# Two transformer blocks with a mixture of experts on one core: norm weights by ScalarE's DMA queue, x turned bank by bank, an expert loader that waits on the work itself, and a gate moved to GpSimd

## The reference

```python
h = rms_norm(x, attn_norm_w)
c_q, c_kv, k_rope, dq, dk, dv, g_mla, g_diff = split(h @ w_in)      # widths 256,256,32, then five times 1024
o_mla  = attention(16 heads, from rms_norm(c_q) @ mla_w_uq and rms_norm(c_kv) @ mla_w_ukv)
o_diff = rms_norm(differential_attention(8 heads, rms_norm(dq), rms_norm(dk), dv), diff_subln_w) * 0.2
merged = sigmoid(g_mla + b1) * o_mla + sigmoid(g_diff + b2) * o_diff
x = x + merged @ w_out
# 16 experts; each takes the 32 tokens that score highest for it
hidden = silu(xe @ w_gate[e]) * (xe @ w_up[e])                      # 1024 -> 2048, xe is 32 rows
x = x + scatter(hidden @ w_down[e] * gate)
# second block
proj = rms_norm(x, norm1_g_2) @ w_in_2      # convolution part, 8 heads of stick-breaking attention, gating unit
y_c = gelu(c_u) * (tril(sgu_w) @ rms_norm(gelu(c_v), sgu_norm_g))   # the gating unit
x = x + concat(y_conv, y_attention, y_c) @ w_out_2
x = x + square(relu(rms_norm(x) @ w_ff1_2)) @ w_ff2_2
x = x + sigmoid(rms_norm(x) @ w_ple_gate_2) * (p_2 @ w_ple_proj_2)
```

## Time and profile before

| | |
|---|---|
| median of 3 runs | 1473.36 us |
| profiled execution | 1473.55 us, of which the span of the core is 1471.8 us |
| PE busy | 1129.7 us, 77% |
| DVE busy | 468.1 us, 32% |
| ACT busy | 374.7 us, 25% |
| POOL busy | 49.0 us, 3% |
| DMA read | 491.52 MB, 335 GB/s over the span |

### The profile page before, as it was taken

One profiled execution on the slowest core, in us unless ns is written; L12 is line 12 of the kernel. 1 busy time (PEld: TensorE's weight loads), 2 busy tenths in 40 slices (PEclk: granted clock), 3 DMA queues, 4 the chain that ended last, 5 costly groups with the idle time before them and its releaser, 6 DMA issues.

```text
span 1471.8 us, 20240 instructions
## 1 busy us (share of the span) xinstructions
PE 1129.7 (77%) x8437; PEld 684.3 (46%) x8437; DVE 468.1 (32%) x879; ACT 374.7 (25%) x623; POOL 49.0 (3%) x107
## 2 busy tenths in 40 slices
PE   9999999965656566656656657566566999999998
PEld 8887887521212212212112122122121688999887
DVE  6988885100000000000000000000000478675546
ACT  6658663100001001001001000000100465465434
POOL 1220120000000000000000000000000020000000
PEclk9999999997878968888798687886887999999999
DMA  8663528999999999999999999999999764555551
GB/s 307 200 245 108 206 87 370 420 426 427 427 426 430 428 428 427 427 429 427 426 430 428 427 427 427 428 428 427 430 427 428 294 186 172 172 184 189 196 186 47
DMA packets 58922, 493.33 MB, mean 335 GB/s; under 512 B 6715, under 2 KB 8309, under 8 KB 34165
## 3 DMA queue, kind: packets, MB, share of 16 engines
q1 hardware_dynamic: 58724, 492.07, 82.4%
q10 hardware_dynamic: 144, 0.52, 0.1%
HBM read 491.52 MB, written 1.05 MB: 335 GB/s over the span
## 4 chain that ended last, share of the span: by engine, by line
DMA 54%; PE 40%; DVE 3%; ACT 1%; issue 1%; SPq 0%; ACTq 0%; DVEq 0%
DMA arena<-in_expert_w_down 19%; DMA arena<-in_expert_w_up 18%; DMA arena<-in_expert_w_gate 17%; PE ps L1927 13%; PE ps L2020 7%; PE ps L1932 7%; PE ps L2374 4%; PE ps L2398 2%; PE ps L1999 1%; PE ps L2190 1%; PE ps L2221 1%; DVE w_split L1199 1%; PE ps L1897 1%; PE ps L2134 1%; PE ps L2109 1%
## 5 line engine op out<-in xcount | busy, mean ns | idle before, releaser
L2374 PE MATMUL ps<-ring,arena 128*32 128x512 f32 x1024 | 168.3, 793 | 115.5 <-DMA ring<-in_expert_w_up 60.1
L2374 PE MATMUL ps<-arena 128*32 128x512 f32 x1024 | 163.2, 772 | 115.4 <-DMA arena<-in_expert_w_up 58.6
L1199 DVE TENSOR_TENSOR w_split<-ring,w_split 128x1024 fp32r<-128x1024 f32 (+3 forms) x178 | 201.9, 1141 | 93.6 <-ACT w_split L765 92.3
L765 ACT ACTIVATE w_split<-ring 128x1024 fp32r<-128x1024 f32 (+3 forms) x178 | 175.2, 991 | 180.5 <-PE ps L1932 126.8
L1651 DVE TENSOR_TENSOR arena<-arena,ps 128x512 f32<-128x512 f32 x16 | 11.0, 688 | 557.8 <-PE ps L2374 557.8
L2374 PEld LDWEIGHTS ps<-ring,arena 128*32 128x32 f32 x1024 | 32.9, 127 | 241.5 <-DMA ring<-in_expert_w_up 101.1
L2374 PEld LDWEIGHTS ps<-arena 128*32 128x32 f32 x1024 | 32.7, 126 | 236.0 <-DMA arena<-in_expert_w_up 96.1
L2020 PE MATMUL ps<-hT_hi,w_split 128*128 128x256 f32 x608 | 111.8, 284 | 0.5 <-ACT w_split L765 0.4
L2398 PE MATMUL ps<-arena 128*32 128x256 f32 x1072 | 81.2, 455 | 32.9 <-DMA arena<-in_expert_w_down 27.8
L2398 PE MATMUL ps<-ring,arena 128*32 128x256 f32 x896 | 69.9, 465 | 43.1 <-DMA ring<-in_expert_w_down 40.1
L2020 PEld LDWEIGHTS ps<-hT_hi,w_split 128*128 128x128 f32 x608 | 95.3, 192 | 2.3 <-issue 1.0
(11 more groups left out here) (360 smaller groups left out, 1379.0 us busy)
## 6 DMA issues: line engine op xcount, KB each, us to landing
ring<-in_expert_w_up SPq DMA_DIRECT2D x36, 2048.0 KB, 36.2
arena<-in_expert_w_gate SPq DMA_DIRECT2D x35, 2048.0 KB, 35.6
ring<-in_expert_w_gate SPq DMA_DIRECT2D x28, 2048.0 KB, 35.9
arena<-in_expert_w_up SPq DMA_DIRECT2D x28, 2048.0 KB, 37.2
arena<-in_expert_w_down SPq DMA_DIRECT2D x25, 2048.0 KB, 37.1
ring<-in_expert_w_down SPq DMA_DIRECT2D x21, 2048.0 KB, 37.1
ring<-in_w_ff SPq DMA_DIRECT2D x32, 1024.0 KB, 5.0
ring<-in_w_in SPq DMA_DIRECT2D x23, 1024.0 KB, 5.0
```

Of the source, the lines that this page charges most:

```text
L765: act.activation(w_split[:, n % WBUFS, 0, 0:cols], slot_view(slot, cols)[:, n % 2, :], ACT.Copy).then_inc(split_hi, 1)
L1199: dve.tensor_tensor(buf[:, 1, :], w, buf[:, 0, :].bitcast(F32), ALU.subtract).then_inc(split_lo, 1)
L2374: m = pe.matmul(ps[j * CAP:(j + 1) * CAP, bank, :], xe[:, kt, :], w[r][:, j * FCOL:(j + 1) * FCOL], start=kt == 0, stop=kt == KT - 1, skip ...
```

## The change

- The norm weight of the first product is loaded by ACT's DMA queue, as its first instruction, and no longer by SP between x and the first weights. PE turns it ahead of x, and turns x bank by bank (both halves of tokens of a bank, then the next bank) and not half by half.
- ACT writes `hT_hi` 0 and 1 before the first weight tile is split, then alternates. DVE likewise.
- The turning of the other weight vectors moves from between `c` and `dq` to behind the fourth tile of `dq`; their copies on DVE move behind `low_parts("dq", 3, 5)`.
- `low_parts("uq0", 0, 1)` moves ahead of the angle computation, and the sum of 2048 squares of `dq` on DVE is cut into two with `low_parts("uq1", 1)` between them.
- `gate_outputs` leaves DVE. POOL does it, as an addition and a multiplication of 1024 elements for each of two column halves.
- SP waits on PE's results themselves (`hO_done`, `tr_done`) for six of the first chunks; PE's waits for its own results go. Chunk 2 is loaded as two parts: 3072 of its 4096 columns once the last head is turned (`hT_done`), the rest once the last head is done.
- The first half of chunk 12 is loaded as two quarters, each freed by its own two matrix products.
- In the gating unit the square moves from ACT to POOL, and ACT splits weight tile 2 of `conv` in its place, ahead of the sigmoids of head pair 0.

```diff
-T1_RELEASES = SLOTS - 2
+T1_RELEASES = 4
+        KEYS, KEY_WORDS = 2, 3072
+        all_heads, merged = (hO_done, DHEADS + HEADS), (tr_done, 4 * TRANSPOSED.index("merge") + 4)
+        FREED_BY = {0: (hO_done, DHEADS), 1: (hO_done, DHEADS + IN_GROUP), KEYS: all_heads, LAST_ARENA: all_heads,
+                    3: merged, HALVED: merged}
...
-                    sp.wait_ge(first_half_used, 1)
-                    sp.dma_start(slot[:, 0:WIDE // 2], source[:, 0:WIDE // 2]).then_inc(first_half_loaded, 16)
+                    for i in range(2):
+                        words = slice(i * WIDE // 4, (i + 1) * WIDE // 4)
+                        sp.wait_ge(first_quarter_used, i + 1)
+                        sp.dma_start(slot[:, words], source[:, words]).then_inc(first_quarters_loaded, 16)
...
+            sp.wait_ge(hT_done, DHEADS + HEADS)
+            sp.dma_start(expert_slot(KEYS)[0][:, 0:KEY_WORDS], chunk_source(0, KEYS)[:, 0:KEY_WORDS]).then_inc(keys_loaded, 16)
...
# POOL
-            pool.sem_inc(od_ready, 1)
+            for c in range(2):
+                pool.wait_ge(gate_ready, HALVES + c + 1)
+                g, od = (b[:, :, c * 512:(c + 1) * 512] for b in (gb, dq))
+                step(pool.tensor_scalar(g, g, 1.0, None, ALU.add))
+                pool.tensor_tensor(od, od, g, ALU.mult).then_inc(od_gated, 2)
...
+            pool.wait_ge(gelu_done, 4)
+            pool.wait_ge(sq_read, 7)
+            gating = cv2.rearrange("p h d -> p (h d)")
+            pool.tensor_tensor(sq[:, 0:HALVES * SGU], gating, gating, ALU.mult).then_inc(sq_ready, 1)
...
# ACT
-            high_parts("c", 0, 2)
+            act.dma_start(vec_rows[0:KT, :], t["attn_norm_w"][0].rearrange("(r c) -> r c", c=P)).then_inc(norm_w_loaded, 16)
             act.wait_ge(vec_ready, 1)
-            high_stage("attn", 0, "attn_norm_w")
+            high_stage("attn", 0, "attn_norm_w", range(0, 2))
+            high_parts("c", 0, 1)
+            high_stage("attn", 0, "attn_norm_w", range(2, 4))
+            high_parts("c", 1, 2)
+            high_stage("attn", 0, "attn_norm_w", range(4, KT))
...
-            act.activation(sq[:, 0:HALVES * SGU], cv2.rearrange("p h d -> p (h d)"), ACT.Square).then_inc(sq_ready, 1)
+            high_parts("conv", 2, 3)
...
# DVE
             low_parts("dq", 3, 5)
+            dve.wait_ge(vec_done, 2)
+            dve.tensor_copy(vec[:, KT:NVEC], ps[:, 6, KT:NVEC]).then_inc(vec_ready, 1)
...
-            diff_sums(0)
+            dve.wait_ge(sq_ready, 1)
+            step(dve.tensor_reduce(ss_d[:, 0:HEADS], sq[:, 0:D].rearrange("p (n d) -> p n d", d=DQK), AX, ALU.add))
             low_parts("uq1", 1)
+            head_sums(0, sq[:, D:2 * D].rearrange("p (n d) -> p n d", d=DQK), ss_d[:, HEADS:2 * HEADS])
...
-                if HEADS - 6 < i <= HEADS - 2:
-                    gate_outputs(i - HEADS + 5)
...
# PE
-            pe.wait_ge(x_loaded, 16)
-            transposes("attn", xs, 0)
             pe.wait_ge(norm_w_loaded, 16)
             pe.transpose(ps[:, 4, 0:KT], vec_rows[0:KT, :], ident[0:KT, 0:KT]).then_inc(vec_done, 1)
+            pe.wait_ge(x_loaded, 16)
+            for b in range(4):
+                transpose_bank(xs, 0, b, range(HALVES)).then_inc(tr_done, 1)
...
+            tiles("dq", hT, range(0, 4))
             pe.wait_ge(vec_loaded, 16 * N_VEC)
-            tiles("dq", hT, range(0, 4))
             pe.wait_ge(c_norm, 4)
             out_of_psum("c")
+            pe.transpose(ps[:, 6, 0:NVEC], vec_rows[:, :], ident[0:NVEC, 0:NVEC]).then_inc(vec_done, 1)
...
-            pe.wait_ge(hO_done, DHEADS)
-            pe.sem_inc(chunk_used, 1)
```

More of the change, by code:

```diff
@@ L1079, in _ @@
             sigmoids(0)
-            high_parts("conv", 2, 3)
             turned_qk(2)
@@ L1290, in _ @@
             low_parts("dq", 7)
+            low_parts("uq0", 0, 1)
             ang, turns, sin_a, cos_a, tmp = trig[:, 0, :], trig[:, 1, :], trig[:, 4, :], trig[:, 5, :], trig[:, 2, :]
@@ L1899, in transpose_bank @@
                 return m
-            def transposes(s, src, base, ready=None):
-                for h in range(HALVES):
-                    if ready is not None:
-                        ready(h)
-                    for b in range(4):
-                        m = transpose_bank(src, base, b, [h])
-                        if h == HALVES - 1:
-                            m.then_inc(tr_done, 1)
             def stage_ready(s, kt=KT - 1):
@@ L2375, in expert @@
                                               start=kt == 0, stop=kt == KT - 1, skip_group_check=True)
-                            if first and bank == 0 and kt == 0:
-                                m.then_inc(first_half_used, 1)
+                                if first and bank == 0 and kt == 0 and j % 2:
+                                    m.then_inc(first_quarter_used, 1)
                         m.then_inc(chunk_used, 1)
```

66 lines of the change are left out of this document (27 added, 39 removed).

## The result

The changed kernel takes 1475.05 us (median of 20 runs, 1474.13 to 1477.88); the kernel before took 1472.88 us on the same chip (20 runs). The ratio is 1.0015 with an interval of 1.0009 to 1.0021: slower by 2.2 us, where I had forecast 0.85 us faster, and above the range I gave (1470.2 to 1474.4 us). The profiled span is 1474.0 us against 1471.8. I follow the 2.2 us from the front to the back.

The account below looks back on a forecast made before the run. The experts' DMA stream at memory rate was taken to bound the kernel, starting when PE reaches the first expert. From 1473.36 us, 0.65 (earlier stream) and 0.2 (second block) came off, giving 1472.5 us; range 1470.2 to 1474.4.

Parts of the forecast that it names:

- The frame: At the first expert: the DMA stream follows PE microsecond for microsecond, and its end is its start plus fixed bytes.
- The start: Kernel's start to ukv0: table load exposed, DVE waits for the turned vectors; PE 1.3 us late at 55.5, bounds 0 to 2.0.
- DVE and POOL side by side ... I take 0, without a row that shows it: Heads with POOL's gates: DVE's splits could slow, costing PE 0 to 0.6 us; taken as 0.
- the 0.6 us that the moved gates were to bring: Last heads: without DVE's merge ahead of the maximum, PE loses its 0.59 us idle at 218.50 and gains 0.6 us.
- POOL's gates slow DVE: Rival, at the heads: POOL's gates cost 0.6 us, time 1473.1 us; chance 0.08.
- PE's own waits: Idles of 0.30 us at 167.78, 224.26 and 228.00 go: PE gains 0.9 us.
- The first quarter is free 0.44 us earlier: Chunk 12: its first part waits for four fewer PE instructions, so the stream starts 0.44 us earlier.
- No hole opens ... I take 0: Chunk 12: a quarter is 1.2 us of DMA, the second is free 0.44 us behind, so no hole opens.
- The early load of chunk 2: Before chunk 12: 3.7 us of DMA come early, but the queue then stands empty; taken as 0. Rival that it pays: 0.08.
- The second block: At conv tile 2: PE gains its 0.39 us wait for ACT's split and gives half back; 0.2 us faster.
- The rival of a late norm weight: At the start: PE waits for the norm weight ahead of x; 1473.4 to 1474.9 us, chance 0.13.
- the further stand of ACT: Rival, at the start: the table load is followed by 1.38 us more on ACT; 1473.9 us, chance 0.06.

Follow-up runs that it names:

- e11: The changed kernel with an early first ACTIVATE on ones alone; 1474.42 us, 1.2 over the kernel before, ratio 1.0008.
- e3: The changed kernel with an early first ACTIVATE and the vector copies moved into the middle of the position calculations; 1473.09 us, ratio 1.0001 to before.
- e10: The kernel before with POOL gating the outputs in two halves as the only change; 1474.28 us, 1.0 over before, ratio 1.0008.
- e7: The changed kernel with the edits of e2 and e3, and POOL's gates in eight pieces of 128 columns; 1470.60 us, ratio 0.9983 to before.
- e12: e9 with chunk 12's first half loaded as two quarters again; 1471.09 us, 2.2 under before, ratio 0.9989.
- e9: e7 with ACT's split of conv tile 2 behind the sigmoids again; 1470.66 us, 2.6 under before, ratio 0.9986.
- e2: The changed kernel with chunk 12 started by one half again in place of two quarters; 1474.97 us, 1.8 over before, ratio 1.0013.
- e6: The changed kernel with the edits of e1, e2 and e3, and chunk 2 loaded whole; 1471.79 us, 1.2 under before, ratio 0.9994.
- e8: e5 with chunk 2 loaded whole, without the early load; 1472.24 us, 0.7 under before, ratio 0.9994.
- e5: The changed kernel with the edits of e1, e2 and e3, and the conv tile 2 split behind the sigmoids again; 1471.14 us, ratio 0.9984 to before.
- e1: The changed kernel with the gates on DVE again in four pieces, none on POOL; 1474.12 us, 1.0 over before, ratio 1.0007.

## Why the prediction was wrong

The sign was wrong: +2.2 us where I had -0.85. The frame held: the stream follows PE at the first expert (the issue of chunk 12 lies 1.08 to 1.15 us behind PE's first product in every kernel where I looked), and the end follows the stream. Two terms failed, one was mis-sized to the other side, and two small gains did not come.

- **The start: right.** "PE is 1.3 us late at 55.5": measured 1.27. The steps in it held too: table load at 6.71 (6.6), hT_hi at 8.01 (7.95), DVE's wait of 1.22 us, cT_lo at 36.76 (37.0). Only dq started at 22.00, not at 22.35. e11 and e3 show that both losses were there to be had back: 1.3 and 0.75 us of PE (ukv0 55.43 and 54.69).
- **"DVE and POOL side by side ... I take 0, without a row that shows it": the step that failed.** With the 0.6 us that the moved gates were to bring, I had -0.6 in the sum; e10 and the changed kernel measure +1.28, an error of 1.9 us. There were two mistakes in it. The first is the duration. I had 3.0 us for a half (1.11 for the addition, 1.90 for the multiplication); the addition took 2.77 us and the multiplication 2.36, so a half takes 5.1 us (in all 11.2 us, over four heads of about 3 us). The second is the exclusion. My bound was two DVE instructions of 0.68 us "slowed by half", and it put the halves beside heads in which PE does not wait for DVE. The instructions that met POOL were the weight splits of 1.2 us, and the row maximum for which PE waits by way of ACT stands behind them. They do not run slower, they stand until POOL's multiplication has ended. The trace of the kernel before shows it, next to the earlier trace rows, where I had read DVE and PE but not POOL. First a split of `conv`, 2.03 us beside POOL's instruction in place of 0.93, and ended 0.82 us behind it:

```profile
1202.43 2.06 POOL L746 TENSOR_TENSOR pT_lo<-arena,pT_hi 128x512 fp32r<-128x512 f32 x1
1203.28 2.03 DVE L1199 TENSOR_TENSOR w_split<-ring,w_split 128x768 fp32r<-128x768 f32 x1
...
1210.57 0.93 DVE L1199 TENSOR_TENSOR w_split<-ring,w_split 128x768 fp32r<-128x768 f32 x1
```

  Then the other way round, POOL standing:

```profile
1208.48 0.20 POOL L692 TENSOR_TENSOR stat<-stat 128x8 f32<-128x8 f32 x1
1208.77 0.24 POOL L693 TENSOR_SCALAR stat<-stat 128x8 f32<-128x8 f32 x1
1209.10 1.56 POOL L694 TENSOR_TENSOR stat<-stat 128x8 f32<-128x8 f32 x1
```

  A POOL instruction on 8 elements takes 1.56 us in place of 0.20 to 0.22 while DVE's scan of two operands (1208.90 to 1210.66) is under way, and it ends with the scan. The Trainium skill, page "SBUF — State Buffer", section "Who interferes with whom", says that a VectorE instruction with two SBUF inputs contends with a GpSimd instruction that reads SBUF, through a port pair that is an exclusive lock, and that the order of issue decides who blocks. The rows here agree in both directions (2.32 and 2.45 us of DVE; 3.74, 1.66 and 1.56 us of POOL); the split of 1.41 us in e7 is the one that stood for less than the POOL instruction ahead of it. With +1.28 in place of -0.6 the forecast would have been 1.0 us over before: the sign turns on this term alone. The rival "POOL's gates slow DVE" had the right pair of engines, but 0.6 us and 8% for it.
- **PE's own waits: mis-sized.** Three idles of 0.30 us went, as said. But from the end of the heads to x's first transposes PE needs 21.91 us in place of 22.90 (before 222.88 to 245.78, now 225.10 to 247.01): 1.0 us for the last two, not 0.6. With the 0.3 of the first that is 1.3 where I had 0.9. The raising of the counter, which "cost nothing visible", has its part in it, presumably; no run separates it. The three terms give 1.27 + 1.28 - 1.3 = 1.25, and PE is 1.23 us late at the first expert.
- **"The first quarter is free 0.44 us earlier": wrong.** The first quarter's counter is raised two products ahead of the half's, not four, or 0.22 us by my own scale, and of that little is seen: the issue stands 1.08 to 1.09 us behind PE's first product in the five kernels with quarters, 1.12 to 1.15 in the nine with a half.
- **"No hole opens ... I take 0": wrong.** Every kernel has the dip right behind the issue. A second one, between 3 and 6 us behind the issue, is in all five kernels with quarters, with 98 to 172 GB/s in its lowest half microsecond; in that stretch none of the nine with a half is under 279. With quarters the 8 us behind the issue run at 290 to 315 GB/s, with one half and the early load at 345 to 351 (five kernels each). From the issue to the marker that is 889.48 to 890.43 us (mean 889.86) against 888.80 to 889.42 (mean 889.05): 0.8 us for the quarters. In the changed kernel's own profile the loss is 0.92. e12 against e9 and e2 against the changed kernel give 0.4 each by the medians (inside the noise), e12 against e9 1.1 by the marker, where e9's profile is a fast one; all ways of counting agree in sign, the size is 0.4 to 1.1.
- **The early load of chunk 2** was worth little, as forecast, but not by the way I gave. I had the queue stand empty before the first quarter; the DMAs still move 475 GB/s from 264 to 265, and the issue is at 265.33. The bytes were given back earlier, in a hole at 249 us, while SP waited for PE to free the ring's places. Its worth is 0.4 to 1.1 us by the medians of e6 and e8 against e5, where I took 0.
- **The second block: 0.2 became 0.** I had DVE's scan give half back; it gives all back (PE's wait of 0.39 for the high split became one of 0.35 for the low). e5 has the 0.25 us, with the split left where it was.

Together: 1.23 (PE late) - 0.03 (issue nearer to PE) + 0.92 (stream) + 0 (second block) = 2.1 us, beside 2.2 measured. That sum is of two single profiles; the 0.92 holds the quarters' 0.8 and the chance of two executions. The rival of a late norm weight did not happen, nor the further stand of ACT (hT_hi starts 1.30 us behind the load's start).

What stays open is why two DMAs of 0.5 MB restart the stream more slowly than one of 1 MB. They are issued 0.4 us apart. Their rows are half as long, and there is one issue more. SP also takes longer over its issues: the one of the chunk's second half takes 1.21 to 1.84 us in four of the five kernels with quarters (in e11 it is the two quarters, 2.07 together) and 0.33 in the nine others. No run tells these apart. Open is also why POOL's addition on 128x1024 takes 2.77 us here and two such 2.22 together at the earlier trace rows.

## What to carry to other kernels

Before work is moved from DVE to POOL, list the DVE instructions with two SBUF operands in that stretch, and count for each up to the whole length of POOL's longest instruction there as a wait. Where the work must go to POOL, cut it into pieces shorter than the slack of the engine beside it: the same gates cost PE 1.3 us in halves, and gave it 0.6 us in eighths (against the gates on DVE). When the first data instruction of an engine gets a second wait ahead of it, look where its table load went, and give it a first instruction without data. And bytes that are loaded early are given back where something later in the queue waits for a place: here 3.7 us of DMA brought 0.4 to 1.1.

## What the runs showed of the hardware

- A DVE instruction with two operands from SBUF and a POOL instruction that reads SBUF held each other up, and either can be the one that stands. A DVE split of 1.2 us took 2.32 and 2.45 beside a POOL multiplication of 2.35, ending 1.08 and 1.09 us behind it (e10: 1.08 for both); a POOL multiplication of 0.73 took 1.66 beside a split of 1.22 (e7). Behind the start of a POOL addition, which reads one operand, a split took 1.41 (e7). The profile counts the stand as duration, not as idle time.
- Behind the first issue of chunk 12 the DMA rate falls in all fourteen profiles, to 66 to 279 GB/s in its lowest half microsecond, and 2.5 us behind it it is back at 279 or more. In e6 and e8, where chunks ahead were still coming in, the fall is smallest (to 246 and 279), but from issue to marker they take 889.22 and 889.80 us, no less than the five with the early load and one half (888.80 to 889.42).
- TensorE's granted clock fell to 0.50 (1.2 GHz) for some 3 us in the router in three of fourteen profiles and cost PE 0.36 to 0.37 us there (e2, e10, e11).
- The first microseconds move the whole kernel. In kernels with the same start (e1, changed, e2) PE began to turn x at 5.70, 5.97 and 5.96 us and took 1.96, 1.97 and 2.39 us for it; it began c at 9.26, 9.54 and 9.95, and its stall of 0.41 us in the mla heads ended at 191.93, 192.23 and 192.61.
